# SSD group norm of a hybrid decoder trunk: the inverse root taken as one power on GpSimd

## The reference

```
y = y.reshape(n, l, SSD_D_INNER) * jax.nn.silu(z)
yg = y.reshape(n, l, SSD_GROUPS, SSD_D_INNER // SSD_GROUPS)
yg = yg * lax.rsqrt(jnp.mean(yg * yg, axis=-1, keepdims=True) + NORM_EPS)
y = yg.reshape(n, l, SSD_D_INNER) * norm_w
```

## Time and profile before

| what | us |
|---|---|
| median of three runs | 1358.43 |
| lowest, highest | 1355.84, 1359.29 |
| the profiled execution's own time | 1357.99 |
| its span, first to last instruction | 1355.9 |
| PE busy in the span | 1305.3 |
| DVE, ACT, POOL busy | 798.9, 631.0, 485.0 |

### The profile page before, as it was taken

The page is one execution under the profiler, slowest core; times in us unless marked ns, Lnnn a source line. Parts: engine busy times, 40 slices in busy tenths (PEclk is TensorE's granted clock), DMA queues, the critical chain, the costliest instruction groups (busy, mean ns, idle before and its releaser), DMA issues. The chain is left out here.

```text
span 1355.9 us, 29088 instructions
## 1 busy us (share of the span) xinstructions
PE 1305.3 (96%) x11346; PEld 1253.9 (92%) x11346; DVE 798.9 (59%) x1570; ACT 631.0 (47%) x1412; POOL 485.0 (36%) x414
## 2 busy tenths in 40 slices
PE   5999999999999999999999999899998999999997
PEld 4999999999999999999999999898997989979997
DVE  4445454553465444645445256576979879697464
ACT  4333342433333433333335264377576766765352
POOL 0555432455323553334642233003334343252031
PEclk9999999999999999999999999899999999999999
DMA  6484333663436643438533174333463735643351
GB/s 193 124 231 119 99 103 111 168 173 92 113 83 182 180 105 85 124 112 260 136 97 90 38 235 123 105 106 111 142 182 111 205 104 156 199 146 109 89 175 67
DMA packets 313544, 182.49 MB, mean 135 GB/s; under 512 B 75248, under 2 KB 302272, under 8 KB 313024
## 3 DMA queue, kind: packets, MB, share of 16 engines
q1 hardware_dynamic: 313408, 180.64, 46.6%
HBM read 155.01 MB, written 46.41 MB: 149 GB/s over the span
## 5 line engine op out<-in xcount | busy, mean ns | idle before, releaser
L1878 POOL TENSOR_TENSOR wlo<-w,whi 128x1024 fp32r<-128x1024 f32 x95 | 228.4, 2404 | 421.1 <-ACT whi L1518 421.1
L1355 PE MATMUL at_proj<-uhi,whi 128*128 128x272 f32 x1536 | 334.3, 299 | 2.5 <-PEq L3032 1.9
L1355 PE MATMUL at_proj<-uhi,wlo 128*128 128x272 f32 x1536 | 318.3, 289 | 0.0
L1355 PE MATMUL at_proj<-ulo,whi 128*128 128x272 f32 x1536 | 318.0, 288 | 0.0
L1518 ACT ACTIVATE whi<-w 128x1024 fp32r<-128x1024 f32 x95 | 100.7, 1060 | 333.1 <-PE at_proj L1355 306.2
L1355 PEld LDWEIGHTS at_proj<-uhi,whi 128*128 128x128 f32 x1536 | 239.8, 190 | 5.8 <-issue 2.2
L1355 PEld LDWEIGHTS at_proj<-ulo,whi 128*128 128x128 f32 x1536 | 242.3, 189 | 0.0
L1355 PEld LDWEIGHTS at_proj<-uhi,wlo 128*128 128x128 f32 x1536 | 241.1, 189 | 0.0
L2363 PE MATMUL kept<-uhi,whi 128*128 128x272 f32 (+1 forms) x744 | 163.4, 300 | 2.7 <-DVE wlo L2763 1.9
L2363 PE MATMUL kept<-uhi,wlo 128*128 128x272 f32 (+1 forms) x744 | 154.7, 289 | 0.0
L2363 PE MATMUL kept<-ulo,whi 128*128 128x272 f32 (+1 forms) x744 | 154.6, 288 | 0.0
(11 more groups left out here) (378 smaller groups left out, 2413.3 us busy)
## 6 DMA issues: line engine op xcount, KB each, us to landing
w<-in_attn_w_in_dram SPq DMA_DIRECT2D x88, 512.0 KB, 4.4
w<-in_ssd_w_in_dram SPq DMA_DIRECT2D x38, 512.0 KB, 4.4
sd_h<-in_state_ssm_dram SPq DMA_DIRECT2D x16, 512.0 KB, 6.8
sd_bc<-acs_p SPq DMA_DIRECT2D x16, 512.0 KB, 5.1
out_s_ssm_dram<-sd_h SPq DMA_DIRECT2D x16, 512.0 KB, 3.3
w<-in_ssd_w_out_dram SPq DMA_DIRECT2D x13, 512.0 KB, 3.7
at_k_cache<-in_cache_kv_w_dram SPq DMA_DIRECT2D x384, 16.0 KB, 2.8
at_v_cache<-in_cache_kv_w_dram SPq DMA_DIRECT2D x24, 256.0 KB, 3.9
```

The lines of the kernel that those rows point to most:

```text
L1355: last = pe.matmul(proj[:, r, h, 0:HALF], a[:, r, kk * P:(kk + 1) * P], b[:, kk, h * HALF:(h + 1) * HALF], start=(kk == 0 and a is whi and ...
L1878: pool.tensor_tensor(wlo[:, r], w[:, r], whi[:, r].bitcast(F32), ALU.subtract).then_inc(wlo_ready, 1)
```

## The change

The mean square plus epsilon is raised to the power -1/2 in one GpSimd instruction for each half, at `SUM`, in place of DVE's reciprocal and ACT's root. DVE sets the exponent, one column, once in the setup. DVE's multiplication at `FN` waits for the same semaphore as before, which GpSimd now raises.

```diff
+        exponent = m.sb("exponent", [P, 1])
...
-                elif what == "FN":
-                    x = var[:, k * HALF:(k + 1) * HALF]
-                    act.wait_ge(inv_ready, 2 * e + k + 1)
-                    act.activation(x, x, ACT.Sqrt).then_inc(rstd_ready, 1)
...
             dve.sem_inc(wlo_ready, PAIR)
+            dve.memset(exponent[:, :], -0.5)
...
                     dve.tensor_scalar(x, bank(item, e)[:, 0:HALF], 1.0 / GW, EPS, ALU.mult, ALU.add).then_inc(var_ready, 1)
-                    dve.wait_ge(var_ready, 2 * e + k + 1)
-                    dve.reciprocal(x, x).then_inc(inv_ready, 1)
...
+                elif what == "SUM":
+                    x = var[:, k * HALF:(k + 1) * HALF]
+                    pool.wait_ge(var_ready, 2 * e + k + 1)
+                    pool.tensor_tensor(x, x, exponent[:, :].broadcast_to([P, HALF]), ALU.pow).then_inc(rstd_ready, 1)
```

## The result

The changed kernel takes 1690.93 us (median of 4 runs, 1689.19 to 1695.13) against 1357.3 before: the ratio is 1.2463, 95% interval [1.2445, 1.2482]. It is 333.6 us slower, far above the range of the forecast, 1355 to 1450.

A forecast was written before the change was run, and what follows sets the result against it. PE, busy 96% of the span, was taken to bound the kernel, with DVE second tight at finishes. Stalls of 8.3, 5.6, 6.7 and 0 us plus 4.5 for the clock gave +25.1 on 1357.99, forecast 1383, range 1355 to 1450.

The forecast's parts named there:

- What comes: Eight GpSimd powers on 128x272, two to a head group's finish, each estimated at 5 us.
- d = 5 us: Duration d of one GpSimd power: twice 2.6 us, the reciprocal's factor of 4.3 applied to POOL; chance 0.50 for 1.8 to 10.
- the upper end: Longest duration considered for one power: about 30 us, from some 50 whole-tile steps of 0.6 us.
- three operations a cycle: GpSimd microcode rate from the Trainium skill; 50 operations at 1.2 GHz over 272 columns give 3.8 us a power.
- d over 10: Rival: a power is a long software routine of 10 us or more; 1422 us at 10, 1454 at 14; chance 0.20.
- Where it lies: Powers in POOL's queue delay YA(0), x_end (3) twice, then nothing at the fourth finish: 8.3, 5.6, 6.7 and 0 us.
- The clock: After each of three PE stalls the granted clock falls, costing some 1.5 us each, 4.5 in all.
- What goes: At the finishes DVE loses eight reciprocals, 14.8 us; ACT loses eight roots and table loads, net 8.5 us.
- costed at nothing: The root's table load moved to L871: free, as ACT waits 0.75 us there anyway; 1.28 us without that cover.
- The 3.4 us of waits: PE idle time behind the reciprocals of the first three finishes, 1.53, 0.82 and 1.03 us, the most that could be won.
- The first rival: A power costs as a plain pass, up to 1.8 us: 1355 to 1361 us, not slower; chance 0.25.
- The third rival: DVE and ACT relief comes through although the power is long, x_end and YA having slack: 1358 us; chance 0.05.

The follow-up runs named there:

- Experiment 5: The changed kernel with the power on only 29 columns of each half, the others keeping the mean square: 1381.17 us, ratio 1.0175.
- experiment 2: The changed kernel without the power, so that reciprocal, root and power are all left out: 1355.24 us against 1356.34, ratio 0.999.
- experiment 1: The changed kernel with a multiplication by the exponent in the power's place, same shape, waits and position: 1355.61 us, ratio 0.9991.
- experiment 3: The changed kernel with the power on half of the columns of each half, 128x136 in place of 128x272: 1518.69 us.

## Why the prediction was wrong

**The step that failed** is the duration under "What comes": d = 5 us, made from DVE's reciprocal (4.3 times a plain pass) times two, with 0.6 and 30 us as ends. It is 43.7 us, above even the upper end, and the forecast's range stopped well short of that end, at d = 13.5. DVE's factor for an iterated operation says nothing of POOL's: there the factor over the multiplication is 68. The upper end, 50 whole-tile passes, took it for granted that one instruction costs less than the same calculation in separate passes; it costs more than that estimate. The prediction's estimate from the Trainium skill's three operations a cycle (GPSIMD Engine Reference, Performance versus the Vector engine), 3.8 us, was off by more than a factor of 11. Nothing in the trace of before bounded the price from above, and the text said so only of d over 10. With only 0.20 on that case, the range was too narrow for an operation of which no row existed.

**Where it lies was right.** With d = 43.7 the formulas, 2d - 1.7, 2d - 4.4, 2d - 3.3 and 2d - 12.2, give 85.7, 83.0, 84.1 and 75.2, together 328.0. Measured: 83.9, 82.9, 85.0 and 76.5, together 328.3. That the sums agree to 0.3 us is in part luck, since each measured term also holds some relief of DVE and some loss to the clock: of the 76.5, the wait itself is 75.4. Experiment 5 shows the same formulas to 1.3 us a term at the forecast's own d. The waits that were named are those that appear: L2894 for POOL in the first finish, L2481 in the second and third, and PE for L2760 in the fourth. In the first finish PE also stops once before, 35.73 us for x_end (2); the sum needed no term for it, since YA(0) ends later.

**The clock.** The term, 1.5 us for each stall, has the right size, but not all of it reaches the total. Busy time by stretch of the changed kernel for the 3 us behind the second and the fourth stall (columns as in rows 2):

```profile
1295.39:1298.39 3.00, 3.00 (x7) 1.87 (x8) 0.91 (x5) 0.00 (x0) 3.00 (x3) 0.51 0.00 0
...
1612.69:1615.69 3.00, 3.00 (x13) 3.00 (x14) 1.57 (x2) 0.66 (x1) 0.00 (x0) 0.50 0.58 174
```

Behind the first and the third it is 0.53 and 0.50. So each time PE runs for some 3 us at its 1.2 GHz level and loses about 1.5 us. Behind the fourth stall, where nothing hides it, the lateness grows by 1.5 us up to L812. From L2481 of the second finish to the first `var` of the third it grows by 0.8, and from L2481 of the third to the first `var` of the fourth by 1.0. Behind the first stall none shows: by the first `var` of the second finish the lateness has fallen from 83.9 to 82.7.

**What goes** was right in its count and wrong in its worth. The eight reciprocals, eight roots and four loads went, and one table load moved to L871 as was said:

```profile
1627.33 1.28 ACT L871 ACT_TABLE_LOAD   x1
1628.62 0.21 ACT L871 ACTIVATE m_stats<-m_stats 128x5 f32<-128x5 f32 x1
```

This load was costed at nothing, because ACT waited there anyway. That is a second, small step that failed: in the last stage DVE and PE wait for the copy behind it, about 1.1 us by L826 (experiment 2), and the last stage is 1.6 us longer in the changed kernel, not far from the 1.28 that the text named if the cover was gone. The 3.4 us of waits behind the reciprocals were taken for the gain; experiment 2 shows 1.1. In part that is the moved load; in part DVE's lead in the first finish ends at a wait for PE and ACT that the old reciprocals had covered. The first rival's case, a cheap operation, was forecast at 1355 for 0.6 us and measured at 1355.6 (experiment 1), though x_end (3) was not in time there, as that text had it: PE waited 0.95 us for it twice. The third rival, slack behind x_end and YA, is ruled out by experiment 3 and, for a short power, by experiment 5, which had to stay under 1367 for it.

## What to carry to other kernels

Before a calculation is moved to another engine by an operation that no row of the profile shows, measure that operation alone: one instruction of the shape wanted, at the end of a kernel that runs anyway, would have told all of this. On an engine whose queue is in order, a long instruction costs its length at each place where the scan's next item is behind it or the result is waited for, and moving it only exchanges the one for the other. Before replacing work by something faster, first leave it out altogether: here that showed 1.1 us (2.6 at most by the interval), which no replacement was likely to be worth. And where a table load moves, follow what is queued behind it: a short wait ahead of it on the same engine was no cover.

## What the runs showed of the hardware that was not expected

- A power on GpSimd costs 0.39 us and 0.159 us for each column, the same for 128, 16 and 1 partitions and for every base and exponent tried. So 544 values on one partition should cost as much as 544 columns of 128, while the same values laid over 128 partitions as 5 columns would be about 1.2 us (0.39 + 5 x 0.159, an estimate). A kernel of that form was not tried: by experiment 2 it had about 1 us to win, and it needs further transposing work from PE.
- The first GpSimd instruction of the pair took 1.0 us more than the second in the first finish: 44.70 against 43.70 in the changed kernel, 5.94 against 4.94 on 29 columns, and 1.62 against 0.64 with the multiplication. So it is not the power's own. The kernel before shows the same on other work of POOL: YA(0) took 1.36 us there, where the changed kernel took 0.46. Its cause is open.
